# Recurrence gates of a streaming encoder: the rounded part and the rest of 64 channels stacked in 128 rows

## What is computed

```python
xc = p["conv_b"] + sum(xpad[:, k:k + T] * p["conv_w"][k] for k in range(CONV_W))
xb = xc.reshape(B, T, LRU_BLOCKS, LRU_BW)          # 8 blocks of 64 channels
r = jax.nn.sigmoid(jnp.einsum("btnc,ncd->btnd", xb, p["w_gate_a"]).reshape(B, T, LRU_W) + p["b_gate_a"])
i = jax.nn.sigmoid(jnp.einsum("btnc,ncd->btnd", xb, p["w_gate_x"]).reshape(B, T, LRU_W) + p["b_gate_x"])
a = jnp.exp(-LRU_C * r * jax.nn.softplus(-p["lru_lambda"]))
b = jnp.sqrt(-jnp.expm1(2.0 * jnp.log(a))) * (i * xc)
h_t = a_t * h_(t-1) + b_t
```

## Time and profile before

| | us |
|---|---|
| median of 3 runs | 2485.27 |
| lowest, highest | 2481.19, 2485.93 |
| profiled execution | 2481.51 |
| its span, first to last instruction | 2479.7 |

### The profile page before, as it was taken

How to read it: one execution, slowest core, us unless ns; L and a number is a source line. 1 busy time by engine, 2 the same in 40 slices (tenths; PEclk the granted TensorE clock), 3 DMA queues, 4 the chain that set the end, 5 groups by cost and what they waited for, 6 DMA issues and landing times.

```text
span 2479.7 us, 43928 instructions
## 1 busy us (share of the span) xinstructions
PE 2458.4 (99%) x17424; PEld 2371.6 (96%) x17424; DVE 1802.2 (73%) x2778; ACT 1220.1 (49%) x2197; POOL 516.0 (21%) x478
## 2 busy tenths in 40 slices
PE   9999999999999999999999999999999999999998
PEld 9999977899999999999999999779999999999997
DVE  7678766579776777677676797674887766776676
ACT  5455355535554454454524653555355544554455
POOL 0024155200112211221201232541001112111222
PEclk9999999999999999999999999999999999999999
DMA  4122201213347635764731222012135467546655
GB/s 155 59 60 72 61 11 38 84 57 110 87 93 137 121 86 102 132 116 89 220 99 52 61 72 61 11 38 89 60 114 99 92 122 130 104 91 117 130 113 172
DMA packets 104537, 230.39 MB, mean 93 GB/s; under 512 B 14816, under 2 KB 17984, under 8 KB 104336
## 3 DMA queue, kind: packets, MB, share of 16 engines
q0 software_dynamic: 43648, 89.14, 20.9%
q1 hardware_dynamic: 60544, 138.42, 17.7%
q10 hardware_dynamic: 144, 0.04, 0.0%
HBM read 144.03 MB, written 81.18 MB: 91 GB/s over the span
## 4 chain that ended last, share of the span: by engine, by line
PE 91%; DVE 4%; DMA 2%; issue 2%; ACT 1%; POOL 0%; SPq 0%; DVEq 0%; ACTq 0%; POOLq 0%
PE ps L959 27%; PE ps L1304 23%; PE ps L1353 20%; PE ps L1168 5%; PE ps L1183 4%; PE ps L1445 2%; PE ps L1238 2%; PE ps L1115 2%; PE ps L1416 1%; DMA raw_all<-in_wst 1%; PE ps L1026 1%; PE ps L1140 1%; PE ps L1047 1%; DVE wlo L2809 1%; DVE raw_all L2941 0%
## 5 line engine op out<-in xcount | busy, mean ns | idle before, releaser
L1974 ACT ACTIVATE whi<-raw_all 128x512 fp32r<-128x512 f32 (+1 forms) x420 | 250.2, 600 | 348.2 <-DVE raw_all L2941 128.0
L2809 DVE TENSOR_TENSOR wlo<-raw_all,whi 128x512 fp32r<-128x512 f32 (+1 forms) x420 | 271.4, 652 | 174.6 <-ACT whi L1974 170.5
L3307 POOL DMA_DIRECT2D x_scratch<-stage x224 | 199.7, 942 | 845.9 <-DVE stage L2951 698.1
L2027 ACT ACTIVATE stage<-ps 128x536 f32<-128x536 f32 (+1 forms) x224 | 135.3, 610 | 110.0 <-PE ps L1353 104.6
L1497 ACT ACTIVATE whi<-raw_all 128x1024 fp32r<-128x1024 f32 (+3 forms) x72 | 66.7, 926 | 236.9 <-PE ps L959 234.4
L2951 DVE TENSOR_TENSOR stage<-stage,ps 128x536 f32<-128x536 f32 (+1 forms) x168 | 118.8, 707 | 85.8 <-PE ps L1353 84.8
L2519 DVE TENSOR_REDUCE mxp<-ps 64x1 f32<-64x64 f32 (+11 forms) x384 | 140.3, 372 | 55.0 <-PE ps L1115 48.4
L959 PE MATMUL ps<-xgh,whi 128*128 128x358 f32 (+1 forms) x720 | 157.3, 327 | 0.0
L959 PE MATMUL ps<-xgl,whi 128*128 128x358 f32 (+1 forms) x720 | 156.6, 325 | 0.0
L959 PE MATMUL ps<-xgh,wlo 128*128 128x358 f32 (+1 forms) x720 | 156.5, 325 | 0.0
L959 PEld LDWEIGHTS ps<-xgl,whi 128*128 128x128 f32 x720 | 124.0, 189 | 0.0
(11 more groups left out here) (835 smaller groups left out, 7680.0 us busy)
## 6 DMA issues: line engine op xcount, KB each, us to landing
raw_all<-in_wst SPq DMA_DIRECT2D x232, 256.0 KB, 3.3
raw_all<-in_wst SPq DMA_DIRECT2D x80, 512.0 KB, 3.6
x_scratch<-stage POOLq DMA_DIRECT2D x112, 268.0 KB, 5.8
x_scratch<-stage POOLq DMA_DIRECT2D x112, 264.0 KB, 5.8
x_scratch<-xall POOLq DMA_DIRECT2D x24, 537.0 KB, 3.6
xall<-x_scratch SPq DMA_DIRECT2D x24, 537.0 KB, 9.4
xall<-in_xT SPq DMA_DIRECT2D x16, 537.0 KB, 7.4
raw_all<-in_wst POOLq DMA_DIRECT2D x30, 256.0 KB, 4.0
```

Source lines behind the costliest of these rows:

```text
L1974: nc.scalar.activation(dst, src, ACT.Copy).then_inc(S["u_hi"], 1)
L2027: nc.scalar.activation(quarters(stage_of(L, g, i, n)[:, 0:N2]), src, ACT.Copy, scale=-1.0 if row else 1.0).then_inc(S["x_copy"], 1)
L2809: V.tensor_tensor(dst, src, hi.bitcast(F32), ALU.subtract).then_inc(S["u_lo"], 1)
L3307: pool.dma_start(x_scr[2 * i + row, :, a:b], stage_of(L, g, i, n)[:, 0:b - a], accum_op=ALU.add).then_inc(S[done], 16)
```

## The change

For the pair of 64-channel blocks of group c, the even block (first 64 rows) and the odd one (last 64) get a tile each. In `x_even` the rows 0 to 63 hold the high part and the rows 64 to 127 the low part of the same 64 channels; in `x_odd` it is the other way round. The weights of a block are both gates side by side, 64 x 128, and stand twice, one above the other. One matmul over 128 rows is then high plus low input for both gates, and two passes (high weights, low weights) do what took three; the product of the two low parts comes along. The even block's result goes to banks 6 and 7 and the free end of the slot's third bank (512, 512 and 48 columns), the odd block's to the slot in three times 358. A group is one unit instead of two, so all the later units are renumbered, and `take` waits for other readers than before. Banks 6 and 7 are shared by all groups: group c waits for the i gate's tanh of group c - 1.

ScalarE makes the high parts with two copies of 64 rows, and each gate with three tanhs of 64 rows (1024, 50 and 1074 columns), VectorE makes the low parts with two subtractions of 64 rows. The order of the queues stays.

```diff
-U_XR, U_GR, U_GATE, U_CKV = [0, 1, 2, 3], [4, 5, 8, 9], [6, 10, 14, 18], [12, 13]
-U_KR, U_CQ = 16, [17, 20, 21, 22, 23, 24]
+U_XR, U_GR, U_GATE, U_CKV = [0, 1, 2, 3], [4, 5, 7, 8], [6, 9, 12, 15], [10, 11]
+U_KR, U_CQ = 13, [14, 16, 17, 18, 19, 20]
...
-    READ[U_GATE[_c]] = ("gate_r", _c + 1)
-    READ[U_GATE[_c] + 1] = ("gate_i", _c + 1)
+    READ[U_GATE[_c]] = ("gate_i", _c + 1)
...
+        def even_gates(c, end):
+
+            rest = ps[:, 3 * slot_of(U_GATE[c]) + 2, CH:CH + end - SUM_END]
+            return (ps[:, 6, :], 0, 512), (ps[:, 7, :], 512, SUM_END), (rest, SUM_END, end)
...
                 def gates(c):
+                    u, b = U_GATE[c], B_GATE[c]
                     w("xc_lo", c + 1)
-                    for k in range(2):
-                        product(to_slot(U_GATE[c] + k), U_GATE[c] + k, B_GATE[c], 128 * k, [tok(xch)], [tok(xcl)])
+                    w("w_lo", b + 2)
+                    take(u)
+                    if c:
+                        w("gate_i", c)
+                    else:
+                        w("root", SUM_MIX)
+                    for i, part in enumerate((whi, wlo)):
+                        for dst, c0, c1 in even_gates(c, TOK):
+                            nc.tensor.matmul(dst, part[b % 2][:, 0:P], x_even[:, c0:c1], start=(i == 0), stop=(i == 1))
+                    for i, part in enumerate((whi, wlo)):
+                        for q in range(3):
+                            mm = nc.tensor.matmul(to_slot(u)(q), part[b % 2][:, P:2 * P], tok(x_odd)(q), start=(i == 0), stop=(i == 1))
+                    mm.then_inc(S["mm"], 1)
...
                     if c:
-                        w("mm", U_GATE[c - 1] + 2)
-                    nc.scalar.activation(xch[:, :], xc[c][:, :], ACT.Copy).then_inc(S["xc_hi"], 1)
+                        w("mm", U_GATE[c - 1] + 1)
+                    for e, dst in ((0, x_even), (1, x_odd)):
+                        ins = nc.scalar.activation(dst[half(e), :], xc[c][half(e), :], ACT.Copy)
+                    ins.then_inc(S["xc_hi"], 1)
+
+                def gate(c, dst, e, bias):
+
+                    rest = even_gates(c, T)[2][0]
+                    nc.scalar.activation(dst[0:64, 0:SUM_END].rearrange("p (c n) -> p c n", c=2), ps[half(e), 6:8, :], ACT.Tanh, scale=0.5,
+                                         bias=bias[half(e), c:c + 1])
+                    nc.scalar.activation(dst[0:64, SUM_END:T], rest[half(e)], ACT.Tanh, scale=0.5, bias=bias[half(e), c:c + 1])
+                    return nc.scalar.activation(chunks(dst[64:128, :]), slot(U_GATE[c])[half(1 - e)], ACT.Tanh, scale=0.5, bias=bias[half(1 - e), c:c + 1])
...
-                    nc.scalar.activation(chunks(t1), slot(U_GATE[c]), ACT.Tanh, scale=0.5, bias=half_ba[:, c:c + 1]).then_inc(S["gate_r"], 1)
+                    gate(c, t1, 0, half_ba).then_inc(S["gate_r"], 1)
...
-                    w("mm", U_GATE[c] + 2)
-                    nc.scalar.activation(chunks(t4), slot(U_GATE[c] + 1), ACT.Tanh, scale=0.5, bias=half_bx[:, c:c + 1]).then_inc(S["gate_i"], 1)
+                    gate(c, t4, 1, half_bx).then_inc(S["gate_i"], 1)
...
             for s in (0, 1):
                 V.memset(ps[:, 3 * s + 2, CH - 2:CH], 0.0)
+                V.memset(ps[:, 3 * s + 2, CH + TOK - 1024:CH + T - 1024], 0.0)
...
                 def xc_lo(c):
                     w("xc_hi", c + 1)
-                    lo(xcl[:, :], xc[c][:, :], xch[:, :], "xc_lo")
+                    V.tensor_tensor(x_even[half(1), :], xc[c][half(0), :], x_even[half(0), :].bitcast(F32), ALU.subtract)
+                    V.tensor_tensor(x_odd[half(0), :], xc[c][half(1), :], x_odd[half(1), :].bitcast(F32), ALU.subtract).then_inc(S["xc_lo"], 1)
```

More of the change, by code:

```diff
@@ L189 @@
 DONE_AT = [CLOSE_DOWN.index((_m, 0)) + 1 for _m in range(8)]
-U_XR, U_GR, U_GATE, U_CKV = [0, 1, 2, 3], [4, 5, 8, 9], [6, 10, 14, 18], [12, 13]
-U_KR, U_CQ = 16, [17, 20, 21, 22, 23, 24]
-U_UQ, U_K, U_V = [25, 26, 27, 28, 29, 30], 31, 35
-U_OY, U_OO, U_MLP = [45 + _c for _c in range(8)], 53, 61
+U_XR, U_GR, U_GATE, U_CKV = [0, 1, 2, 3], [4, 5, 7, 8], [6, 9, 12, 15], [10, 11]
+U_KR, U_CQ = 13, [14, 16, 17, 18, 19, 20]
+U_UQ, U_K, U_V = [21, 22, 23, 24, 25, 26], 27, 31
+U_OY, U_OO, U_MLP = [41 + _c for _c in range(8)], 49, 57
 NU = U_MLP
@@ L244 @@
     LAST_UNIT[B_GR[_c]] = U_GR[_c]
-    LAST_UNIT[B_GATE[_c]] = U_GATE[_c] + 1
+    LAST_UNIT[B_GATE[_c]] = U_GATE[_c]
     LAST_UNIT[B_OO + _c] = U_OO + 2 * _c + 1
@@ L460, in trunk @@
         xch, xcl = tiles("xcs", "X", 6, 2, F32R)
+        x_even, x_odd = xch, xcl
         sqa, sqt = tiles("sqa", "X", 6, 2)
@@ L3386 @@
             put(B_GR[c], block(w_in[:, s3 + P * c:s3 + P * c + P]))
-            gate = np.zeros((P, 2 * P), f32)
-            for n, name in enumerate(("w_gate_a", "w_gate_x")):
-                for i in range(2):
-                    gate[64 * i:64 * i + 64, P * n + 64 * i:P * n + 64 * i + 64] = a[name][l, 2 * c + i]
-            put(B_GATE[c], gate)
+            even = [a[name][l, 2 * c] for name in ("w_gate_a", "w_gate_x")]
+            odd = [a[name][l, 2 * c + 1] for name in ("w_gate_x", "w_gate_a")]
+            put(B_GATE[c], np.tile(np.concatenate(even + odd, 1), (2, 1)))
         for c in range(2):
@@ L3436 @@
         parts = [cols(a["norm_mix_g"][l]), cols(a["q_norm_g"][l]), cols(a["kv_norm_g"][l]), cw, cols(a["conv_b"][l]), cols(a["b_gate_a"][l]),
-                 cols(a["b_gate_x"][l]), cols(a["lru_lambda"][l]), cols(a["attn_out_g"][l]), cols(a["lru_out_g"][l]), cols(a["norm_mlp_g"][l]),
+                 np.roll(cols(a["b_gate_x"][l]), P // 2, 0), cols(a["lru_lambda"][l]), cols(a["attn_out_g"][l]), cols(a["lru_out_g"][l]), cols(a["norm_mlp_g"][l]),
                  cols(a["norm_mix_g"][min(l + 1, DEPTH - 1)])]
```

## The result

| | before | changed |
|---|---|---|
| median, us | 2485.27 | 2523.01 |
| lowest to highest, runs | 2481.19 to 2485.94, 5 | 2517.64 to 2525.35, 5 |
| profiled execution, us | 2481.51 | 2524.3 |
| its span, us | 2479.7 | 2522.5 |

The changed kernel is slower: ratio 1.0156, 95% interval 1.0145 to 1.0167, so 38.8 us (36 to 42). The forecast was 2510 with a range to 2520. Direction and chain were right, the size was too small: 42.8 us between the two profiled executions, where my steps gave 24.6. Some 4 to 5 of the 42.8 us are their place among the runs: the profiled execution of the kernel before lies 3.8 us under its median, that of the changed kernel 1.3 us over its own.

A forecast was written before the change was run, and what follows sets the result against it. VectorE's queue was to pace the gate groups at 28.6 us although TensorE is 99% busy: 18.5 us to group 3, 6.0 behind it and 0.1 for memsets make 24.6, added to 2485.3 for 2510 us, range 2497 to 2520.

The forecast's parts named there:

- What the change removes: TensorE gate groups: 18 matmuls become 12, 3.17 us becomes 2.05; 4.4 us saved a layer, 8.8 in both.
- What it adds on ScalarE and VectorE: Per group: gate tanhs 2.4 us more, high copy 1.0, low subtraction 1.2, first tanh 0.57 later; recurrence 17.3 us behind group.
- Rival 2: ScalarE and VectorE: 64 rows cost about half of 128; 2482 us, no change; chance 0.06.
- GpSimd's hold-up: GpSimd's gelu cube delays VectorE behind the recurrence; added cost between 0 and 1.5 us per group, 0.4 taken.
- Whether that is hidden: Not hidden: groups 28.6 us apart, TensorE waits some 2.9, 2.9 and 6.6 us; 18.5 us later over both layers.
- Clock: TensorE behind the waits: a fall to 1.2 GHz would cost 0 to 13.9 us a layer; nothing taken in the sum.
- rival 3: Clock falls in the 6 us waits: 2 to 4 us more a layer, 2514 to 2518 us; chance 0.2.
- the prediction's own sign of being wrong: Wrong if the recurrence started under 15 us behind its group, GpSimd's added hold-up exceeded 1.5 us, or granted clock sank.
- Behind group 3: From group 3 to the query products: 3.1 us later less 0.1 a layer, 6.0 us in two layers.
- Rival 1: Chains of ScalarE and VectorE are hidden and only the passes count: 2476.5 us; chance 0.04.

The follow-up runs named there:

- the halves in the kernel before: Kernel before with its three passes, but each gate tanh, the high copy and the low subtraction in two 64-row pieces; 2504.21 us, ratio 1.0079.
- The run with the clock kept up: Changed kernel plus 9, 10 and 25 dummy matmuls of 512 columns ahead of gate groups 1, 2 and 3; 2514.07 us, ratio 1.0132.
- the kernel with the high copy first: Changed kernel with the next channels' high copy ahead of the r gate's pieces and their low subtraction ahead of a split; 2501.98 us, ratio 1.0073.
- the kernel with the sum's low part first: Last of four further queue orders: query latent 1's emptying, a split and the key latents' low part before the last recurrence's scans; 2492.81 us.

## Why the prediction was right or wrong, point by point

**What the change removes: right.** Group 0 takes 82.92 - 81.26 = 1.66 us to its last row, and three matmuls of 358 columns step by 0.49 us elsewhere: 2.15 us, 2.05 forecast.

**What it adds on ScalarE and VectorE: right, some tenths short.** The changed kernel's ScalarE at group 0, first the three pieces of tanh r and the tanh behind, then the two copies; and VectorE's subtractions and the products behind them:

```profile
83.61 1.11 ACT L1541 ACTIVATE t<-ps,half_ba 64x1024 f32<-64x1024 f32 x1 [1.03 <-PE ps L1026]
84.63 0.28 ACT L1543 ACTIVATE t<-ps,half_ba 64x50 f32<-64x50 f32 x1
84.92 1.15 ACT L1544 ACTIVATE t<-ps,half_ba 64x1074 f32<-64x1074 f32 x1
86.11 1.28 ACT L1555 ACTIVATE t<-t,sp 128x1074 f32<-128x1074 f32 x1
...
94.47 2.19 ACT L1535 ACTIVATE xcs<-xc 64x1074 fp32r<-64x1074 f32 x2
```

```profile
96.69 1.27 DVE L2281 TENSOR_TENSOR xcs<-xc,xcs 64x1074 fp32r<-64x1074 f32 x1 [5.78 <-ACT xcs L1535]
97.98 1.27 DVE L2282 TENSOR_TENSOR xcs<-xc,xcs 64x1074 fp32r<-64x1074 f32 x1
99.28 2.06 DVE L2288 SCALAR_TENSOR_TENSOR t<-t,t 128x1074 f32<-128x1074 f32 x1
101.38 3.05 DVE L2290 SCALAR_TENSOR_TENSOR t<-t,xc 128x1074 f32<-128x1074 f32 x1
```

The pieces take 86.11 - 83.61 = 2.50 us for 2.4 forecast (1.19 in the earlier trace rows), and VectorE's subtractions follow at 1.29. The recurrence starts 99.28 - 81.26 = 18.0 us behind its group, forecast 17.3: 0.2 us of this are the tanhs' pieces, 0.2 the subtractions, 0.1 the start of the first tanh. Rival 2, that 64 rows cost half, is ruled out by these lines and by the halves in the kernel before. GpSimd's hold-up is on the first two products now (2.06 and 3.05 us for 1.28 each), 2.55 us, within the forecast's bounds: from the recurrence to group 1 it is 110.43 - 99.28 = 11.15 us, forecast 11.35. It grew by 0.1 and not 0.4, because the kernel before lost more than the 1.7 us of its split: the short scan of the same recurrence, 0.26 us elsewhere, was held up too.

```profile
99.42 1.05 DVE L2265 TENSOR_TENSOR_SCAN xc<-t,h0s,t 128x34 f32<-128x34 f32 x1
```

ScalarE is busy 30.0 us more (27 forecast), VectorE 19.0 (10 forecast; its 8 more subtractions are 10.2 of them).

**Whether that is hidden: right.** The waits ahead of groups 1, 2, 3 are 2.63, 3.67, 6.26 us, forecast 2.9, 2.9, 6.6, at the named instructions. The first distance, the only one that starts from a warm group, is 29.17 for 28.6. These 0.57 us three times a layer are 3.4 of the 18 us missing, the smaller of the two terms that were short.

**Clock: this is the step that failed.** I took nothing in the sum, since no row showed a fall, and kept the fall as rival 3 with 0.2, behind the 6 us waits alone and at 2 to 4 us a layer. The clock fell to 1.2 GHz behind all three waits, in both layers, and the prediction's own sign of being wrong, a granted clock that sinks, came true. A cold group takes 2.0 us longer, and a long wait ahead of the next group doesn't hide them, because the chain starts from the group: ScalarE's tanhs must wait for its last matmul. So the recurrence of group 2 starts 161.61 - 141.63 = 20.0 us behind its group instead of 18.0, and the next distance is 31.3 instead of 29.2. What the product behind the group loses at half clock lies in the next wait and costs nothing of its own.

```profile
161.61 2.20 DVE L2288 SCALAR_TENSOR_TENSOR t<-t,t 128x1074 f32<-128x1074 f32 x1
```

That is 2.0 us in the second distance, 2.0 in the third, and 2.0 behind group 3, which is most of the 2.4 and 2.6 us in the row "group 3 to the key latents' squares": 6 us a layer, 12 in both. The run with the clock kept up got 8.9 us back by the medians and 11.1 by the parts of the two profiled executions, with a wait of 1.15 us of its own ahead of group 2: 9 to 12 us, where the sum had nothing. The Trainium skill, "TensorE: Matmul & The Clock Gate", section "Why this matters for your kernels", warns that idle gaps between bursts of matmuls bring the clock back to half; the trace agrees, at 0.50 behind a wait of 2.63 us. I had the rule beside the sum, and judged it by waits of at most 1.3 us, which could not speak against it. And I overlooked that the trace of the kernel before does show a fall. Its last matmul ends at 2468.05 us, and the view of waits doesn't count the idle time behind it; the page's last slice, of 62 us, still shows a 9. The stretches of that end (TensorE's busy time first, then the others' and the clock as above):

```profile
2468.00:2471.00 3.00, 0.05 (x1) 0.00 (x0) 3.00 (x9) 2.40 (x4) 0.00 (x0) 1.00 0.80 298
2472.00:2479.00 7.00, 0.00 (x0) 0.00 (x0) 2.11 (x6) 0.00 (x0) 0.00 (x0) 0.50 0.91 282
```

The clock is at full until 2471 and at half from 2472, 3 to 4 us behind the last matmul. The wait of 6.6 us that I forecast ahead of group 3 was longer, so the fall there could have been read before the change; for those of 2.9 us this row says nothing.

**Behind group 3: right but for the clock.** From the squares of the key latents to those of y 2.7 and 2.5 us, forecast 3.0.

**Rivals.** Rival 1, that only the passes count, is refuted twice. TensorE waits at every group behind the first, so the chains are not hidden, and even with nothing added the 8.8 us of passes bring nothing that can be measured (some 3 us at most by the interval), since VectorE's and ScalarE's chain to group 3 has almost no air either. Rival 3 came true in mechanism and exceeded its price, some 5.5 to 6 us a layer for 2 to 4, because it counted the waits of 6 us alone.

With the two missing terms the sum is 24.6 + 3.4 + 12 = 40.0 of the 42.8 us of the profiled executions. The remaining 2.8 us were not traced to an instruction; the runs of one kernel lie further apart than that (2481.2 to 2485.9 us before).

## What to carry to other kernels

An engine that is busy 99% of the time is not the only bound: a second chain of engines that runs beside it with little air (here 3.9 us ahead of group 1 and 0.15 ahead of group 3) counts with all that it grows beyond this air, and where it doesn't get shorter, it keeps the first engine from gaining what that saves. Before an operand is packed for TensorE, count the instructions that pack and unpack it, because halving the rows of an instruction on ScalarE or VectorE halved nothing here (1.27 us for 1.28). And when a forecast opens waits of some microseconds ahead of matmuls, price what stands behind them at half clock, and count it in full where the chain that sets the next distance starts from it. The end of a trace, where TensorE has finished, can show that the clock falls.

## What the runs showed of the hardware

How long TensorE waits doesn't alone say whether its clock falls. In the profiled executions it was 0.50 behind waits of 2.31, 2.56, 2.63, 3.67, 3.76, 4.06, 4.60 and 6.26 us, and stayed at 1.00 behind 1.94 us and less. But the kernel with the high copy first has nearly the same wait in both layers, ahead of query latent 0, and ran on at full steps behind it in the first layer and at half clock in the second. The timeline there:

```profile
148.63 0.73 PE L965 MATMUL ps<-xgh,whi 128*128 128x358 f32 x3 [3.17 <-ACT t L1544]
149.20 0.65 PE L965 MATMUL ps<-xgl,whi 128*128 128x358 f32 x3
...
1392.56 1.13 PE L965 MATMUL ps<-xgh,whi 128*128 128x352 f32 x3 [3.19 <-ACT t L1544]
1393.49 1.08 PE L965 MATMUL ps<-xgl,whi 128*128 128x352 f32 x3
```

Nor need the fall come with the first matmul behind the wait: in the kernel with the sum's low part first, the first query product starts at nearly full steps (0.60 us from 222.32 to 222.92), and from 223.0 to 226.4 the granted clock is 0.50, with steps of 0.89:

```profile
222.92 0.99 PE L965 MATMUL ps<-cql,whi 128*128 128x358 f32 x3
223.71 1.09 PE L965 MATMUL ps<-cqh,wlo 128*128 128x358 f32 x3
224.60 1.09 PE L965 MATMUL ps<-cqh,whi 128*128 128x358 f32 x3
```

What decides between them the runs don't show. And GpSimd's hold-up of VectorE moves with the order of the queue: 2.55 us on two products in the changed kernel, 0.9 and 2.2 us on the two scans of the last recurrence in the last order. It was smaller where VectorE stood idle beside the cube anyway: in the last order the recurrence of group 2 loses 0.9 us, on its last product (2.17 for 1.28), and VectorE then waits 1.38 us for TensorE.
